# Running the FFN down projection, the final norm and the second block's first norm and projections in one region, with both norm factors multiplied in at the evictions

## What is computed

```python
    h = rmsnorm(x, norm_ffn)
    x = x + conv_glu_ffn(h, f_up, f_conv_w, f_conv_b, f_down)
    x = rmsnorm(x, norm_final)
    # second block
    h = rms_norm(x, g_norm)
    proj = h @ w_in            # q_a, k_a, v_a, q_i, k_i, w_i, z_a, ... , k_rope, ...
    # q_a, k_a: normed per head and rotated;  q_i, k_i: rotated;  then the top-k attention
    # ... and at the end  x = x + merged @ w_out
```

## Time and profile before

| what | value |
|---|---|
| median of 3 runs (lowest, highest) | 1973.21 us (1972.74, 1975.27) |
| the profiled execution: its time | 1971.63 us |
| its span in the profile | 1969.8 us |
| TensorE busy, share of the span | 88% |
| VectorE, ScalarE, GpSimd | 43%, 35%, 37% |
| mean granted TensorE clock | 0.934 |

### The profile page before, as it was taken

The page is one execution under the profiler, slowest core; times in us unless marked ns, Lnnn a source line. Parts: engine busy times, 40 slices in busy tenths (PEclk is TensorE's granted clock), DMA queues, the critical chain, the costliest instruction groups (busy, mean ns, idle before and its releaser), DMA issues. The chain is left out here.

```text
span 1969.8 us, 25467 instructions
## 1 busy us (share of the span) xinstructions
PE 1738.7 (88%) x10348; PEld 1308.9 (66%) x10348; DVE 848.4 (43%) x1439; ACT 698.8 (35%) x1182; POOL 728.4 (37%) x380
## 2 busy tenths in 40 slices
PE   5999978889998999998993997889787979987999
PEld 4866648858776888887883773554565446875777
DVE  4658764448424364332004105865411765223222
ACT  4334442234425323222122322324534345344431
POOL 4423323316440355545442445210133520452342
PEclk9999989979999999999996998978888889988999
DMA  4311110014330323332332220100113010332131
GB/s 158 132 58 60 54 54 4 4 56 139 97 96 11 96 86 96 96 96 81 96 102 80 80 92 11 60 27 6 49 39 105 0 43 17 112 99 105 54 102 58
DMA packets 39428, 138.56 MB, mean 70 GB/s; under 512 B 4368, under 2 KB 5648, under 8 KB 38288
## 3 DMA queue, kind: packets, MB, share of 16 engines
q1 hardware_dynamic: 39312, 136.93, 21.8%
HBM read 132.72 MB, written 4.19 MB: 70 GB/s over the span
## 5 line engine op out<-in xcount | busy, mean ns | idle before, releaser
L352 POOL TENSOR_TENSOR parts<-ring,parts 128x1024 fp32r<-128x1024 f32 (+3 forms) x251 | 569.3, 2272 | 958.7 <-ACT parts L343 958.4
L390 PE MATMUL banks<-h_hi,parts 128*128 128x512 f32 x1096 | 476.6, 435 | 34.4 <-ACT a_gate L570 9.8
L391 PE MATMUL banks<-h_lo,parts 128*128 128x512 f32 x1096 | 439.3, 401 | 0.0
L392 PE MATMUL banks<-h_hi,parts 128*128 128x512 f32 x1096 | 438.5, 400 | 0.0
L343 ACT CAST parts<-ring 128x1024 fp32r<-128x1024 f32 (+3 forms) x251 | 245.2, 980 | 247.7 <-PE banks L392 231.0
L390 PEld LDWEIGHTS banks<-h_hi,parts 128*128 128x128 f32 x1096 | 210.8, 192 | 118.6 <-issue 63.2
L391 PEld LDWEIGHTS banks<-h_lo,parts 128*128 128x128 f32 x1096 | 211.0, 193 | 56.5 <-issue 12.6
L392 PEld LDWEIGHTS banks<-h_hi,parts 128*128 128x128 f32 x1096 | 210.9, 192 | 49.2
L2156 DVE TENSOR_TENSOR x<-x,banks 128x512 f32<-128x512 f32 x16 | 11.0, 687 | 155.6 <-PE banks L392 155.6
L390 PE MATMUL banks<-ffn_act_hi,parts 128*128 128x512 f32 x176 | 69.3, 394 | 5.5 <-PEq L279 5.5
L2540 ACT CAST ffn_act_hi<-ffn_gate 128x512 fp32r<-128x512 f32 x22 | 13.7, 621 | 167.1 <-DVE ffn_gate L2488 167.1
(11 more groups left out here) (528 smaller groups left out, 3123.4 us busy)
## 6 DMA issues: line engine op xcount, KB each, us to landing
ring<-weights SPq DMA_DIRECT2D x211, 512.0 KB, 3.5
ring<-weights SPq DMA_DIRECT2D x24, 256.0 KB, 2.6
ring<-weights SPq DMA_DIRECT2D x8, 384.0 KB, 3.0
x<-xT SPq DMA_DIRECT2D x2, 1024.0 KB, 6.3
x<-xT SPq DMA_DIRECT2D x1, 2048.0 KB, 7.6
x_spill<-x SPq DMA_DIRECT2D x1, 2048.0 KB, 6.3
x<-x_spill SPq DMA_DIRECT2D x1, 2048.0 KB, 8.2
outT<-x SPq DMA_DIRECT2D x8, 256.0 KB, 2.0
```

Source lines behind the costliest of these rows:

```text
L352: self.nc.gpsimd.tensor_tensor(self.parts[:, t % PARTS, 1, 0:w], self.ring[:, t % SLOTS, 0:w], self.parts[:, t % PARTS, 0, 0:w].bitcast(F3 ...
L390: nc.tensor.matmul(out, w.hi, x.hi, start=first, stop=False)
L391: nc.tensor.matmul(out, w.hi, x.lo, start=False, stop=False)
L392: return nc.tensor.matmul(out, w.lo, x.hi, start=False, stop=last)
```

## The change

One stage takes the place of four. `add_and_glu` goes on after f_up with the 8 f_down jobs and 13 more; the norm_final stage, the second `Norms` and the `project` stage are gone. The 13 jobs come as a_qi, a_small, a_qk, and read the FFN's h buffer, which is filled tile by tile with x (before any norm) times norm_final times g_norm_2. Two sums of squares are built beside f_down, of x and of x times norm_final; from them come root (1/rms of x) and step (1/rms of the normed x), and their product `factor`, `[P, S]`, is multiplied in by VectorE as each bank is taken out (`take`). Meanwhile x itself is normed, stored to DRAM in two halves, and the k.h that later stages need is written from it. Job banks go round 6, not 7; banks 6 and 7 hold the sums.

```diff
@@ weight_plan
-    feats("a_qk", w2, C_QA, 1024)
     feats("a_qi", w2, C_QI, 512)
     plan.append(("a_small", ...
+    feats("a_qk", w2, C_QA, 1024)
@@ conv_glu
-        add_to_x(k, "f_down", act_t, FT, 3)
@@ add_and_glu
+    def taken_before(pe, job):
+
+        if job >= LATER:
+            job -= LATER
+            pe.wait_ge(*(G("added").ge(DT + job + 1) if job < DT else G("bank_taken_dve").ge(job - DT + 1)))
+        elif job == 0:
+
+            pe.wait_ge(*G("value_taken").ge(FT))
@@ SP
-            k.prefetch(sp, k.used)
+            k.prefetch(sp, in_first + 2)
+            for half, landed in enumerate(k.x_spilled):
+                part = slice(half * DT // 2, (half + 1) * DT // 2)
+                sp.wait_ge(*G("normed").ge((half + 1) * DT // 2))
+                sp.dma_start(k.x_spill[:, part, :], k.x[:, part, :]).then_inc(landed[0], 16)
+                k.prefetch(sp, in_first + 4 if half == 0 else k.used)
+                if half == 0:
+                    start.rope.sp(sp)
@@ PE
+            for m in range(DT):
+                taken_before(pe, m)
+                feature_major(act_t, FT)(k, pe, down_first + 3 * m, later_bank(m), None if m else ActReady(k))
+            for t in range(13):
+                taken_before(pe, DT + t)
+                emit_arriving(k, pe, h, in_first + t, later_bank(DT + t), None if t else Arrived(G("h_low"), DT))
+                if t == 0:
+                    second.pe_sums(pe, (7, 6))
@@ DVE
+            for m in range(DT):
+                dve.wait_ge(k.tile_used, down_first + 3 * (m + 1))
+                nc.vector.tensor_tensor(k.x[:, m, :], k.x[:, m, :], later_bank(m), ALU.add).then_inc(*G("added").inc())
+                second.dve_tile(dve, m)
+
+            def take(t):
+                if t in (5, 9):
+
+                    dve.wait_ge(*k.x_spilled[(t - 5) // 4])
+                dst = start.qi[:, t, :] if t < 4 else start.y[:, 2, :] if t == 4 else k.x[:, t - 5, :]
+                dve.wait_ge(k.tile_used, in_first + t + 1)
+                nc.vector.tensor_tensor(dst, later_bank(DT + t), second.factor, ALU.mult).then_inc(*G("bank_taken_dve").inc())
+
+            second.dve_first(dve, chain, 6)
+            second.dve_x(dve, range(0, 4))
+            second.dve_second(dve, chain)
+            take(0)
+            take(1)
+            second.dve_x(dve, range(4, 8))
+            take(2)
+            take(3)
+            for m in range(DT):
+                second.dve_whole(dve, m)
+                if m % 2:
+                    second.dve_low(dve, m - 1)
+                if m == 3:
+                    take(4)
+            take(5)
+            take(6)
+            start.rope.dve(dve)
+            for t in range(7, 13):
+                take(t)
@@ ACT
+            for m in range(DT):
+                k.split_high(act, down_first + 3 * (m + 1) + LEAD)
+                second.act_tile(act, m)
+            k.split_high(act, in_first + 2 + LEAD)
+            second.act_first_root(act, 7)
+            k.split_high(act, in_first + 3 + LEAD)
+            second.act_second_root(act)
+            k.split_high(act, in_first + 5 + LEAD)
+            for m in range(DT):
+                second.act_whole(act, m)
+                if m == 3:
+                    k.split_high(act, in_first + 6 + LEAD)
+            k.split_high(act, in_first + 7 + LEAD)
+
+            act.wait_ge(*G("bank_taken_dve").ge(5))
...
+            k.split_high(act, in_first + 9 + LEAD)
+            start.rope.act(act)
+            k.split_high(act, k.used + LEAD)
@@ class SecondNorm
+    def act_tile(self, act, m):
...
+        act.wait_ge(*G("added").ge(DT + m + 1))
+        nc.scalar.mul(self.early.hi[:, m, :], k.x[:, m, :], self.gain(m)).then_inc(*G("h_high").inc())
...
+        nc.scalar.activation(self.squares[0] if m else self.totals[0], k.x[:, m, :], ACT.Square).then_inc(*G("squared").inc())
+        nc.scalar.activation(self.squares[1] if m else self.totals[1], k.x[:, m, :], ACT.Square,
+                             scale=k.vec("norm_final", m)).then_inc(*G("squared").inc())
+    def dve_first(self, dve, chain, bank):
+        k, nc, G = self.k, self.k.nc, self.k.counter
+        dve.wait_ge(*G("rooted").ge(2))
+        chain(nc.vector.reciprocal(self.root, self.root))
+        dve.wait_ge(*G("summed").ge(3))
+        chain(nc.vector.tensor_tensor(self.step, self.root, k.banks[bank], ALU.mult))
+        nc.vector.tensor_tensor(self.step, self.step, self.root, ALU.mult).then_inc(*G("mean_ready").inc())
@@ sparse_branch
-                norm_stage(k, [(D, [(k.x[:, t, :], k.x[:, t, :], P, k.vec("norm_final", t)) for t in range(DT)])],
-                           room=merged, beside=RopeTables(k, index_ctx, "freq_a", cos[:], sin[:], sg))
...
-                project(k, jobs, rms_norm(k, index_ctx, k.x, k.h, "g_norm_2", room=sg),
-                        before=lambda sp: sp.dma_start(k.x_spill, k.x[:]).then_inc(k.spilled, 16))
```

More of the change, by code:

```diff
@@ L2561, in _ @@
             high(act, FT - 1)
+            act.wait_ge(*G("gains_ready").ge(1))
+            for m in range(DT):
[12 more added lines that the diff above has]
+            act.wait_ge(*G("bank_taken_dve").ge(5))
+            small = start.y[:, 2, :]
+            for half in range(2):
+                nc.scalar.copy(start.ki[half * AHD:(half + 1) * AHD, :], small[0:AHD, :])
+            nc.scalar.copy(start.wiT[:], small[AHD:AHD + AH, :])
+            nc.scalar.copy(k.rope_key, small[P - BROPE:P, :])
+            k.split_high(act, in_first + 9 + LEAD)
+            start.rope.act(act)
+            k.split_high(act, k.used + LEAD)
         def low(pool, f):
@@ L2575, in _, with __init__, ge @@
             low(pool, FT - 1)
+            k.split_low(pool, in_first + 5 + LEAD)
+            for m in (1, 3):
+                second.pool_low(pool, m)
+            k.split_low(pool, in_first + 6 + LEAD)
+            for m in (5, 7):
+                second.pool_low(pool, m)
+            k.split_low(pool, k.used + LEAD)
+class Arrived:
+    def __init__(self, count, before):
+        self.count, self.before = count, before
+    def ge(self, n):
+        return self.count.ge(self.before + n)
 def emit_arriving(k, pe, x, t, bank, arrivals):
@@ L2591, with __init__ @@
 class RopeTables:
[L2594 removed]
+    def __init__(self, k, ctx, freq, cos, sin, room, raw=None):
         self.k, self.freq, self.cos, self.sin = k, freq, cos, sin
[L2596 removed]
+        self.raw = k.sbuf(ctx, k.fresh("pos_raw"), [P, S], I32)[:] if raw is None else raw
         self.pos, self.turns = room[:, 0, :], room[:, 1, :]
     def sp(self, sp):
[L2600 removed]
+        self.k.load_small(sp, self.raw, self.k.positions.to_broadcast([P, S]))
     def dve(self, dve):
@@ L2800, in close_branch, with sparse_branch @@
                 first_act=gating.act_gates)
-def sparse_branch(k, merged):
+def sparse_branch(k, merged, start):
     nc = k.nc
-    with ExitStack() as ctx:
-        y, z, sg = k.sbuf(ctx, "a_y", [P, 4, S]), k.sbuf(ctx, "a_z", [P, 4, S]), k.sbuf(ctx, "a_gate", [P, DT, S])
-        with ExitStack() as at_ctx:
+    with start.branch as ctx:
+        y, z = start.y, start.z
+        sg = k.sbuf(ctx, "a_gate", [P, DT, S], high=True)
+        with start.at as at_ctx:
             qk = k.x
[L2809 to L2818, removed]
-                norm_stage(k, [(D, [(k.x[:, t, :], k.x[:, t, :], P, k.vec("norm_final", t)) for t in range(DT)])],
-                           room=merged, beside=RopeTables(k, index_ctx, "freq_a", cos[:], sin[:], sg))
[L2822 to L2838, removed]
-                project(k, jobs, rms_norm(k, index_ctx, k.x, k.h, "g_norm_2", room=sg),
-                        before=lambda sp: sp.dma_start(k.x_spill, k.x[:]).then_inc(k.spilled, 16))
@@ L2841, in sparse_branch @@
+            v = k.sbuf(at_ctx, "a_v", [P, ST, AH * AHD], high=True)
+            chosen = k.sbuf(at_ctx, "a_chosen", [P, ST, S], high=True)
+            q_scale = k.sbuf(at_ctx, "a_q_scale", [P, ST, AH], high=True)
+            with start.index:
+                qi, ki, wi, wiT, cos, sin = start.qi, start.ki, start.wi, start.wiT, start.cos, start.sin
                 project_tokens(k, "a_v", k.h, S, lambda act, t, b: nc.scalar.copy(v[:, t, :], b))
```

140 lines of the change are left out of this document (119 added, 21 removed).

## The result

The changed kernel takes 1927.40 us (median; 1922.46 to 1933.53), the kernel before 1974.24 (1972.74 to 1975.40): ratio 0.9773, 95% interval 0.9758 to 0.9788. It is faster by 2.3%. The prediction was 1930.5 us, 1926 to 1938. The profiled execution took 1929.16 us, against 1929.9 in the sum.

The account below looks back on a forecast made before the run. TensorE was taken to set the end, idling in a 38.7 us hole of two norms on VectorE. Gains 2.3 + 38.7 + 0.8 - 1.7 + 1.6 = 41.7 us off 1971.63 give 1929.9; forecast 1930.5, range 1926 to 1938.

Parts of the forecast that it names:

- Term 1: Between f_up and f_down: the gap falls from 5.49 to 3.2 us, 2.3 us gained, with f_down kept at 121.55.
- Terms 2 to 5: After f_down: hole 38.7 us gained, 13 jobs' pace 0.8 gained, two sums 1.7 lost, last stage end 1.6 gained.
- The stretch: From f_up's end to a_v's start: 242.0 us before, expected to come to 200.3, with the kernel's time following.
- The covers: Work costed at nothing because TensorE's jobs hide it, such as the factor, ready at T (f_down's end) + 21 us.
- rival (a): In the 13 jobs: VectorE, put back by GpSimd's splits, holds the sums or factor; 1931 to 1934 us, chance 0.09.
- the two-input rule: A VectorE instruction with two SBUF inputs and a GpSimd instruction reading SBUF exclude each other; 44 such instructions, 18 before.
- so 14 us of cover: Factor ready at T (f_down's end) + 21, bank first needed at job 6, T + 35; lateness beyond costs one for one.
- The table load: Before the next head norm: an added 1.28 us load on ScalarE falls in idle time; nothing, at most 1.3 us.
- (b): In the 13 jobs: ScalarE's roots and TensorE's banks wait in a circle; 5 to 12 us, 1935 to 1942, chance 0.10.
- (c): In the 840 matmuls in one run: the granted clock falls and stays low; slower than before, up to 1992, chance 0.03.
- (d): Behind the region: the hole is not what was waited for and half is given back; 1951 us, chance 0.04.

Follow-up runs that it names:

- dose3: The changed kernel with three more reciprocals of 3.35 us in VectorE's chain ahead of the factor: 1934.78 us, ratio to the kernel before 0.9806.
- h_lower: The changed kernel with top-of-SBUF buffers at multiples of 128 bytes and the FFN's h 32 KB lower, below weight ring and x: 1928.84 us, ratio to before 0.9775.
- down_only: The kernel before, with f_down taken into f_up's stage and nothing else changed: 1971.64 us, ratio to the kernel before 0.9996.
- wait_root: The changed kernel, but the two sums precede the first job and TensorE waits for VectorE's products with the first root: 1936.45 us (one run).
- dose6: The changed kernel with six added reciprocals, 20.1 us, in VectorE's chain ahead of the factor: 1942.93 us (one run).
- early_down: The changed kernel, but f_down's jobs 0, 1 and 2 each wait for their own bank, not the last value bank: 1925.23 us, ratio to before 0.9751.
- early_lower: The changed kernel with f_down's first three jobs waiting for their own banks and h aligned to 128 bytes, 32 KB lower: 1921.59 us, ratio to before 0.9737.
- best: The changed kernel with f_down's first three jobs waiting for their own banks and every buffer split for TensorE at a multiple of 256 bytes: 1911.21 us.
- act_off: The changed kernel with ffn_act's halves starting 96 bytes past a multiple of 256: 1934.49 us, ratio to the kernel before 0.9803.
- h_256: The changed kernel with every buffer allocated from the top of SBUF starting at a multiple of 256 bytes: 1916.70 us, ratio to before 0.9709.

## Why the prediction was right

**Term 1, f_up to f_down.** The gap was 3.21 us, 3.2 said, by the mechanism named: VectorE's product at 919.26 took 1.86 us beside GpSimd's split. f_down was kept at 121.55 and took 122.58. This is the term that was mis-sized, by 1.0 us: the change had 11 steps of 0.43 us at the 1.2 GHz level where the kernel before had 6 (13 and 8 with the steps at both edges, the count that the prediction used). In the eight profiled executions with a gap of 3.2 us in front of f_down the number of such steps was 0 (dose3, h_lower) to 12 (down_only, wait_root, dose6), and it was 0 in the three with a gap under 1 us (early_down, early_lower, best). Behind the same gap f_down took 119.99 to 122.71 us (act_off, with its slower step, apart): the clock's price is no constant. The weak point was to take over the number of one execution.

**Terms 2 to 5.** The hole went whole: the first projection starts within f_down's last matmul (1044.32). The 13 jobs with the two sums took 74.51 us from T to the end of the last (1118.99), 72.8 + 1.7 said. The stage end was 1.05, as said. The stretch came to 201.35 where 200.3 was said, and the missing 1.05 is f_down.

**The covers.** The factor was ready at T + 22.7 where T + 21 was said. The four products on x alone make 1.9 of this, 4.91 us where 3 were reckoned, beside GpSimd's split at 1058.61; the chain ahead of them was 0.5 early and the last product 0.3 over. This is rival (a)'s mechanism (the Trainium skill, "SBUF — State Buffer", "Who interferes with whom", weighed in the prediction), in the place where it costs nothing. More was held than the two-input rule in the prediction covers: in the cos and sin tables a product with one tensor input took 2.51 us, and lasted until GpSimd's split was through, where the next product took 0.43:

```profile
1089.22 2.58 POOL L352 TENSOR_TENSOR parts<-ring,parts 128x1024 fp32r<-128x1024 f32 x1
...
1089.58 2.51 DVE L2732 TENSOR_SCALAR cos_a<-a_y,consts 128x512 f32<-128x512 f32 x1
1092.13 0.43 DVE L2734 TENSOR_SCALAR a_y<-cos_a 128x512 f32<-128x512 f32 x1
```

The step "so 14 us of cover; if it is gone, each microsecond of lateness costs one" was wrong, without changing the time. It counted from the factor to the first bank that TensorE needs back. That cover is 11.9 us (dose6). A nearer one was not seen: factor, normed h, ScalarE's casts of it, and behind them in ScalarE's queue the weight cast of tile 9. It has about 7.3 us (dose3).

**The table load** before the head norm ran at 1152.30, and ScalarE then stood idle for 2.69 us, waiting for TensorE: no cost, as said.

**Rivals.** (b), a circular wait, did not occur. By dose3 it was some 7 us of added work away. (c): the clock stayed at 1.00 in the jobs. (d): from a_v's first matmul to the end it was 808.07 us before and 807.34 after, so nothing was given back.

**The time.** Of the profiled executions' 42.5 us, 40.6 are in the stretch, 1.1 ahead of it and 0.7 behind. The median fell by 46.8. The 4 us between are no effect of the change that a trace shows: its code lies behind f_up, and f_up's end varies by more than this, as the last section tells. So the mechanism and the sum for the stretch are what was right. That the profiled execution came within 0.8 us of the sum, and the median of four runs from 1922.46 to 1933.53 within 3.1 us of what was said, is in part luck.

## What to carry to other kernels

A norm whose factor is one number per token need not stand between two matmul stages: feed the matmuls the unnormed value and multiply the factor in at the evictions. Then ask what the late factor holds up through queues, the weight casts behind it on ScalarE too, and not only when the first bank is needed. Start each moving operand at a multiple of 256 bytes (shown here for fp32r matmuls of 128x512), and let a job wait for its own bank, not for the last one.

## What the runs showed of the hardware that was not expected

**The moving operand's start address sets a matmul's pace.** 128x512 fp32r matmuls, mean from start to start at the 2.4 GHz level: 226.7 ns where both halves start at a multiple of 256 bytes, 232.4 at 128 past one, 233.3 at 96 past one (act_off) and at 224 (the h of the change). It was shown in both directions, by h_256 and act_off, with the tensor's place otherwise kept to some hundred bytes. A third tensor bears it out: the mixer's h starts 192 past a multiple of 256 in the change and steps by 233.3 ns; best puts it on a multiple, 64 bytes higher, and it steps by 226.9. Why 64, 96 and 128 bytes off cost nearly the same is open.

**The time ahead of the change wanders.** In eight profiled executions (before, down_only, the change, early_down, wait_root, dose3, dose6, act_off) no code differs up to f_up's end (act_off has ffn_act at another address); it came at 915.48 to 922.76 us. f_up itself took 247.41 us in each. Already the mixer's output projection (the first matmul that reads y_parts) started at 493.0 to 500.4, so the wandering lies ahead of that, and its 7 us are more than the effects of 1 to 6 us studied here. Its cause was not looked for. Small edits are to be read from the stretch that they touch.

**A shorter wait can make the next one longer.** In h_256 a faster TensorE moved a VectorE instruction of 0.55 us onto GpSimd's split, where it took 2.56.
